# One hybrid decoder layer on one core: two blocks fewer, and the routed rows read back in three groups

## The reference, cut to what matters

```
P = x @ W_in                              # columns for three branches and three gates
A: RWKV-7 recurrence, 8 heads x 64        # S_t = S diag(w) - ..., y_t = S r_t
B: GLU -> causal conv of 31 taps -> LN -> silu
C: attention, 4 heads x 128, into 256 memory rows
h = LN(alpha*x + (sum_b sigmoid(G_b) * y_b) @ W_out)
score = sigmoid(h @ w_router); idx = top_8(score + bias) of 128 experts; gate = 2.5 * normed score
y = LN(alpha*h + shared(h) + sum_{k in idx} gate_k * w_e2[k] @ (silu(h @ w_e1[k]) * (h @ w_e3[k])))
```

## Time and profile before

| | |
|---|---|
| median of 3 runs | 1992.39 us (1991.35 to 1992.70) |
| profiled execution: its own time, its span | 1992.53 us, 1990.8 us |
| granted TensorE clock, mean | 0.951 of full |
| projections, from the span's start | to 319 us |
| recurrence | 326 to 455 us |
| merge | 455 to 753 us |
| first products of expert pair 0 / of pair 63 | 850.5 / 1901.5 us |
| final stage | 1920.8 to 1990.8 us |
| busy: TensorE, VectorE, ScalarE, GpSimd | 1783.4, 627.2, 392.3, 365.0 us |
| moved by DMA | 532 MB, mean 267 GB/s |

### The profile page before, as it was taken

One profiled execution on the slowest core, in us unless ns is written; L12 is line 12 of the kernel. 1 busy time (PEld: TensorE's weight loads), 2 busy tenths in 40 slices (PEclk: granted clock), 3 DMA queues, 4 the chain that ended last, 5 costly groups with the idle time before them and its releaser, 6 DMA issues. The chain is left out here.

```text
span 1990.8 us, 29270 instructions
## 1 busy us (share of the span) xinstructions
PE 1783.4 (90%) x10614; PEld 1047.1 (53%) x10614; DVE 627.2 (32%) x1516; ACT 392.3 (20%) x918; POOL 365.0 (18%) x529
## 2 busy tenths in 40 slices
PE   8999997998999999999988888888888888888887
PEld 6857776887778885645433333333333333333332
DVE  1387754873214312611211111111111111111127
ACT  0114544552120101311111111111111111111112
POOL 1000000888871000011110101111111111111100
PEclk8999998999999999999998989998989898989998
DMA  4443312011233324479999999999999999999965
GB/s 120 147 141 102 97 46 49 3 35 36 79 119 109 119 76 190 198 283 420 421 420 410 419 405 410 419 414 398 411 408 396 411 410 396 413 410 417 409 284 241
DMA packets 160782, 532.04 MB, mean 267 GB/s; under 512 B 22061, under 2 KB 88927, under 8 KB 110205
## 3 DMA queue, kind: packets, MB, share of 16 engines
q1 hardware_dynamic: 138921, 488.47, 62.3%
q0 software_dynamic: 20640, 41.23, 5.5%
q10 hardware_dynamic: 1148, 1.34, 0.2%
HBM read 522.52 MB, written 41.42 MB: 283 GB/s over the span
## 5 line engine op out<-in xcount | busy, mean ns | idle before, releaser
L1944 PE MATMUL bank<-arena 128*64 128x512 f32 x2048 | 513.6, 659 | 139.0 <-DMA arena<-in_w_e 137.8
L1944 PEld LDWEIGHTS bank<-arena 128*64 128x64 f32 x2048 | 159.0, 151 | 489.1 <-issue 487.7
L1962 PE MATMUL bank<-arena 128*64 128x512 f32 x1024 | 233.8, 598 | 0.0
L2187 DVE TENSOR_TENSOR arena<-bank,arena 128x256 f32<-128x256 f32 x64 | 27.2, 425 | 579.1 <-ACT arena L2032 579.1
L1812 POOL DMA_INDIRECT arena<-h_rows,index x66 | 67.1, 1016 | 772.1 <-DVE index L2061 714.2
L1431 PE MATMUL bank<-arena 128*128 128x276 f32 x768 | 184.7, 399 | 7.3 <-ACT arena L1533 3.1
L1431 PEld LDWEIGHTS bank<-arena 128*128 128x128 f32 x768 | 146.5, 191 | 41.6 <-ACT arena L1533 3.5
L2032 ACT ACTIVATE arena<-bank 128x256 f32<-128x256 f32 x64 | 24.7, 386 | 604.5 <-PE bank L1944 604.5
L1201 PE MATMUL bank<-arena 64*64 64x64 f32 (+2 forms) x2816 | 119.6, 239 | 16.4 <-DVE arena L1300 8.7
L1962 PEld LDWEIGHTS bank<-arena 128*64 128x64 f32 x1024 | 67.8, 136 | 110.9 <-issue 109.7
L1201 PEld LDWEIGHTS bank<-arena 64*64 64x64 f32 x2816 | 105.0, 135 | 22.7 <-DVE arena L1300 9.0
(11 more groups left out here) (333 smaller groups left out, 1842.3 us busy)
## 6 DMA issues: line engine op xcount, KB each, us to landing
arena<-in_w_e SPq DMA_DIRECT2D x384, 1024.0 KB, 14.2
arena<-in_w_in SPq DMA_DIRECT2D x50, 512.0 KB, 4.2
arena<-routed_rows SPq DMA_DIRECT2D x8, 2048.0 KB, 23.0
arena<-in_w_mem_kv SPq DMA_DIRECT2D x4, 1024.0 KB, 5.7
arena<-in_cache_mem_k SPq DMA_DIRECT2D x8, 512.0 KB, 4.8
arena<-in_cache_mem_v SPq DMA_DIRECT2D x8, 512.0 KB, 5.5
arena<-in_w_out SPq DMA_DIRECT2D x2, 2048.0 KB, 12.6
arena<-in_w_s SPq DMA_DIRECT2D x3, 1024.0 KB, 10.7
```

Of the source, the lines that this page charges most:

```text
L1944: mm = pe.matmul(p_gu[t * S:(t + 1) * S, :], xt[:, v, c, t * S:(t + 1) * S], w13[2 * v + t][:, :, c, :], start=(c == 0), stop=(c == KD - 1))
L1962: mm = pe.matmul(p_y[h][t * S:(t + 1) * S, :], hidT[:, j, t * S:(t + 1) * S], w2[2 * v + t][:, j, h * 512:(h + 1) * 512], start=(j == 0), ...
```

## The change

**The block.** `stage_front` becomes `front_programs`, whose five programs (unchanged but for two added signals) run at the head of the block of `stage_front_to_experts`. `recycle` and two barriers go. Explicit waits take the barrier's place:

```diff
-            pool.memset(masks[:, 3:5, :], 1.0)
+        pool.memset(masks[:, 3:5, :], 1.0).then_inc(sem("masks_ready"), 1)
...
-                    act.activation(before[:, :, 0:SEQ], rate[:, :, 0:SEQ], ACT.Exp, scale=-RATE)
+                act.activation(before[:, :, 0:SEQ], rate[:, :, 0:SEQ], ACT.Exp, scale=-RATE).then_inc(sem("decays_ready"), 1)
...
     def gpsimd(pool):
+        pool.wait_ge(sem("sample_rows"), 1)
         pool.memset(yout[:, :, SEQ:NT], 0.0)
...
+        pe.wait_ge(sem("masks_ready"), 1)
+        pe.wait_ge(sem("sample_rows_copied"), 6)
         for n in range(NCH):
             chunk(n, n % 2)
...
+        dve.wait_ge(sem("decays_ready"), 1)
         for x in range(4):
             vectors(0, 0, x)
+        dve.wait_ge(sem("masks_ready"), 1)
         chunks(dve, chunk)
...
             wkv_gpsimd(pool)
+            pool.wait_ge(m.sem("state_turned"), 1)
+            pool.wait_ge(m.sem("state_rows"), 1)
+            pool.wait_ge(m.sem("state_done"), 4 * NCH + 4)
+            for name in FRONT_ONLY:
+                pool.sem_clear(m.sem(name))
+            pool.drain()
+            pool.sem_inc(s_cleared, 1)
             pool.wait_ge(m.sem("rwkv_ready"), 1)
```

```diff
-EARLY_GROUPS = ((0, 0, 3), (0, 1, 7))
+EARLY_GROUPS = ((0, 0, 3), (0, 1, 7), (0, 2, 6))
...
+        sp.wait_ge(s_oh, 1)
+        sp.dma_start(w2s, io["w_s2"][0].rearrange("(k p) n -> p k n", p=P)).then_inc(sem("shared_down_loaded"), 16)
...
+        sp.wait_ge(s_base, 2 * NTT + 17)
+        sp.wait_ge(s_out[1], (16 * NP // 2) * count)
+        low(0)
+        sp.wait_ge(s_xt, NP * count)
+        low(1)
+        low(2)
+        sp.wait_ge(s_out[0], (16 * NP // 2) * count + 16)
+        low(3)
+        sp.wait_ge(s_gu, NP * count)
+        for i in range(NTT - 1):
+            ranks(i, O_MID, 4, 2, s_mid)
+        sp.wait_ge(s_out[1], (16 * NP // 2) * count + 16)
+        high(0)
+        high(1)
+        sp.wait_ge(s_in[1], (16 * NP // 2) * count + 16)
+        high(2)
+        sp.wait_ge(s_xt, NP * count + 1)
+        high(3)
...
+        pe.wait_ge(s_rc, NTT)
+        shared(0, 2)
+        shared(1, 2)
         count = rounds(pe)
...
-                    if v == 0:
-                        with pe.If((NP // 2) * r + i < 3):
-                            shared_late(1, i * THIRD, i + 2)
-                    else:
-                        with pe.If((NP // 2) * r + i < 4):
-                            with pe.If(i > 2):
-                                shared_late(0, 2 * THIRD, 5)
+                    with pe.If((NP // 2) * r + i < 13):
+                        if v == 0:
+                            with pe.If(i < 7):
+                                with pe.If(i > 3):
+                                    shared_late(i)
+                        with pe.If(i > 7):
+                            pe.wait_ge(s_base, 2 * i + (v + 1))
+                            for t in range(NTT):
+                                with pe.If(i < 9 + t):
+                                    with pe.If(i > 7 + t):
+                                        base(t, v)
...
+        pe.wait_ge(s_idx, NP * count + 3)
+        pe.wait_ge(s_xt, NP * count + 1)
+        pe.wait_ge(s_hc, NP * count)
+        pe.wait_ge(s_yv, NP * count + 1)
+        pe.wait_ge(s_ya, NP * count + 1)
+        for i in range(NTT - 1):
+            fold(i, O_LOW, 2, s_low)
+        for i in range(NTT - 1):
+            fold(i, O_MID, 1, s_mid)
+            fold(i, O_HIGH, 1, s_high).then_inc(s_all, 1)
```

More of the change, by code:

```diff
@@ new lines, in gpsimd @@
+    def gpsimd(pool):
+        pool.memset(restart, 1.0)
+        pool.drain()
+        pool.memset(restart[:, 0:SEQ:CH], 0.0).then_inc(sem("restart_ready"), 1)
+        pool.wait_ge(sem("key_cache_turned"), BS)
+        pool.drain()
+        for u in range(2):
+            pool.tensor_copy(qri[u][:, :, 2, :], m.fold[:, :].rearrange("p (o c) -> p o c", o=1).to_broadcast([P, KW, HD]))
+        pool.wait_ge(sem("sample_scores"), BS)
+        for h in range(2):
+            r = slice(h * HD, (h + 1) * HD)
+            pool.drain()
+            pool.tensor_copy(masks[r, 0, :], m.lower[r, r])
+            pool.drain()
+            pool.tensor_copy(masks[r, 1:3, :], m.upper[r, :, r])
+        pool.drain()
+        pool.memset(masks[:, 3:5, :], 1.0).then_inc(sem("masks_ready"), 1)
@@ L1042, in _ @@
[L1042 to L1054 removed]
+                last = dve.tensor_tensor(squares[:, j, :], kkey[:, j, :], kkey[:, j, :], ALU.mult)
@@ L1057 @@
+        n_before = TAPS - SCAN_AT
+        for k in range(n_before):
+            tap(k)
+        for q in range(N_STEP):
+            shift(q)
+            maxima(q)
+            if q < SCAN_AT:
+                tap(n_before + q)
+            normalise(q)
+            prepare(q)
+        dve.drain()
+        for j in (2, 3):
+            bonus(j)
+    return sync, gpsimd, tensor, scalar, vector
 O_SOUT = O_TOP + 2 * WEXP - KW * P
@@ L1873, in shared, with shared_late, base, fold @@
             j, third, bank = EARLY_GROUPS[g]
-            mm = shared_half(x, j, third * THIRD, bank)
+            mm = shared_half(x, j, third * THIRD, O_HT, bank)
             if x == 1:
-                mm.then_inc(s_sh, 1)
-        def shared_late(j, first, done):
-            pe.wait_ge(s_sa, done)
-            shared_half(0, j, first, 7)
-            shared_half(1, j, first, 7).then_inc(s_sh, 1)
+                mm.then_inc(s_sh, 1 + g // 2)
+        def shared_late(i):
+            pe.wait_ge(s_sa, i + 3)
+            shared_half(0, 1, i * THIRD, O_HT - 4 * THIRD, 7)
+            shared_half(1, 1, i * THIRD, O_HT - 4 * THIRD, 7).then_inc(s_sh, 1)
+        def base(t, h):
+            n, cols = RES_ROWS[t], slice(t * P, (t + 1) * P)
+            bank = m.ps[7][0:n, :]
+            for j in range(2):
+                pe.matmul(bank, sact[:, j, cols] if n == P else ssam[:, j, :], w2s[:, j, h * 512:(h + 1) * 512],
+                          start=(j == 0), stop=False)
+            for k in range(4):
+                mm = pe.matmul(bank[:, k * P:(k + 1) * P], hT[:, 4 * h + k, cols] if n == P else hsam[:, 4 * h + k, :], alpha,
+                               start=False, stop=(k == 3))
+            mm.then_inc(s_bp, 1)
+        def fold(i, place, n, s):
+            pe.wait_ge(s[i], 32)
+            for h in range(2):
+                for k in range(n):
+                    for a in range(2):
+                        part = m.at(place[i][a], n * D)
+                        mm = pe.matmul(final_bank(i, h)[a * HD:(a + 1) * HD, :], fold64,
+                                       part[:, k * D + h * 512:k * D + (h + 1) * 512],
+                                       start=(place is O_LOW and k == 0), stop=(place is O_HIGH))
+            return mm
         def find_slots(g, n, v):
@@ L2241, in _ @@
         def _(pe):
+            front_tensor(pe)
             wkv_tensor(pe)
@@ L2427, in build @@
             stage(nc, m, io)
-            if stage is stage_front:
-                m.recycle(FRONT_ONLY)
 def kernel(**inputs):
```

1484 lines of the change are left out of this document (730 added, 754 removed).

## The result

The changed kernel takes 1971.91 us (median of 4 runs, 1969.14 to 1978.12) beside 1992.34 us for the kernel before; the ratio is 0.9903, 95% interval 0.9879 to 0.9926. It is faster by 19 us (15 to 24), inside the range, but by two thirds of what was forecast. The profiled execution has a span of 1970.6 us, 20.2 less than before.

A forecast was written before the change was run, and what follows sets the result against it. The prediction took the expert loop as bound by its DMA weight stream, with gains only around it: -8.5 + 0.3 + 1.7 - 24.3 = -30.8 us from 1992.5, forecast 1962 us, range 1953 to 1975.

The forecast's parts named there:

- The boundary: Between projections and recurrence: without the two barriers and with the clears moved, the recurrence starts sooner; -8.5 us.
- Rival B: Samples' recurrence on GpSimd binds and the merge waits: boundary worth only 3 us, 1967 us; chance 10%.
- GpSimd gains 3 us: Samples' recurrence at the boundary: its reload can't start before 321, where it started at 324.46, so GpSimd gains 3 us.
- The stream's start: Ahead of the expert loop: two added matmul sets delay the first weights' request, partly regained; net +1.7 us.
- The tail: Behind the expert loop: a DMA queue, then a VectorE chain; last output at 1966.5 instead of 1990.8, -24.3 us.
- First high tile (1 MB): +2.4, 1931.7: In the tail: the first tile's high ranks land 2.4 us after the reads ahead of them, at 1931.7.
- 1902 + 4 x 0.59 = 1904.4: In the tail: end of the last weights before the change, taken from the DMA share of 0.59 from 1902 to 1906.
- the fold: In the tail: TensorE adds the first high tile in four matmuls of 0.43 us each, 1.7 us.
- Rival A: In the tail: rank reads in flight with pair 63's last weights delay them, end moves by 9 us, 1971; chance 15%.
- Rival C: In the tail: high ranks land early, low and middle ranks fitting under pair 63; up to 11 us less, about 1954; 7%.
- Rival D: In the expert loop: jumps over added code cost TensorE time beyond its room, up to 2005 us; 5% slower, 3% no difference.
- the rule on instruction fetch: TensorE's branches: taken jumps outside two pages of code would force a DMA fetch; the forecast's sum counts them as free.

The follow-up runs named there:

- e1_old_boundary: The changed kernel with the old boundary between projections and recurrence (two barriers, the clears between them): 1982.5 us, ratio 0.9952 to the kernel before.
- e3_high0_alone: The changed kernel with SP waiting until tile 0's high ranks have landed before issuing those of tiles 1 to 3 and the samples: 1972.3 us.
- e5_mids_behind: The changed kernel with the middle ranks of tiles 1 to 3 issued behind tile 0's high ranks, each before its tile's high ranks: 1963.2 us.
- e6_both: The changed kernel with e5_mids_behind's order of reads, and VectorE adding each tile before norming the previous one: 1963.7 us.
- e10_samples_second: As e6_both, with the samples' rows read right behind tile 0's high ranks and normed second: 1964.6 us.

## Why the prediction was right, and where it was not

- **Sign and place.** The gain came from the boundary and the tail, and the stretch of the loop gave next to nothing, as argued. The sum was 11 us too large (31 for 19 to 20), and the tail, one of its terms, accounts for all of that.
- **The boundary, forecast -8.5 us.** The start of the recurrence came 7.3 us sooner within the program (forecast 7.4), at full clock. Over eleven traces the gain up to the samples' turn in the merge is 8.2 us; the direct comparison of medians gives 11.0, with an interval of 4 to 21 that holds both. The clears beside the merge cost nothing that shows.
- **Rival B (GpSimd binds)** didn't come: in every run TensorE turned the samples' rows without an idle before it, 4.8 us or more after GpSimd had asked for them. The step "GpSimd gains 3 us" was too low for the profiled execution: GpSimd asked at 587.2 us instead of 596.7, 9.4 us sooner, and the slack grew instead of shrinking. From the turn of the rows to that request it took 271.8 to 277.1 us in the variants, e1_old_boundary among them with 276.4, and 281.7 before; what makes it differ is open.
- **The stream's start, forecast +1.7 us.** +4.1 up to the first pair, -2.2 inside the loop: +1.9. The first pair ran at full clock, 7.09 us for 8.75.
- **The tail, forecast -24.3 us, measured -13.0.** The step that failed is "First high tile (1 MB): +2.4, 1931.7". Less the 7.2 us by which the last pair came sooner, that is 1924.5; it landed at 1934.9, 10.4 us later. I had ended the weights where the mean share of 16 engines fell, "1902 + 4 x 0.59 = 1904.4", and had not read on: two engines worked until 1914. Whatever is read behind the weights lands by those two. The fourteen others kept to the forecast (e3_high0_alone); the lag is worth some 8 us, and the reads behind the tile another 2. A second and smaller slip is the fold: 3.7 us at half clock instead of 1.7, because TensorE had stood idle for 9.1 us. VectorE's five tiles took 29.6 us instead of 30.8, and the output 2.3 as reckoned. 10.4 + 2.1 - 1.2 = 11.3, which is the difference between -24.3 and -13.0.
- **Rival A (the reads hold up the last weights)** gave 1971, which the measured 1971.9 meets by luck and not by its mechanism: the wait ahead of the last pair was 1.09 us (1.65 before), and holding the reads back didn't shorten it.
- **Rival C (the high ranks land early)** didn't come: they landed 10.4 us late.
- **Rival D and the rule on instruction fetch.** TensorE's loop with ten more guarded pieces shows hardly an idle but the waits for weights (123.7 us of the 125.1 ahead of the pairs' products and 0.5 elsewhere; 137.8 of 139.0 before), and from the first pair to the last it took 1048.75 us instead of 1050.95. By the rule of the Trainium skill (Runtime: NRT & Kernel Launch, "Instruction fetch mechanics") the jumps over the added code could have cost a fetch each; in this loop none shows. What removing the blocks' jumps gained can't be told from what removing their barriers gained.

## What to carry to other kernels

When reads follow a long saturated stream, read the DMA share on until it is zero, not only to where it falls: here a transfer landed when the slowest of its engines was done. Order such reads by what is needed first, and keep everything else behind it. Work put ahead of a bound stream costs most of its length, however much room there is inside it.

## What the runs showed of the hardware

- Two of the 16 DMA engines end some 8 us behind the others: behind the weights in the kernel before (share 0.12 for 8 us), in the variants (0.13 for 7 and for 8 us), and behind the changed kernel's own last reads (0.13 from 1938 to 1944 us). The packet records show two packets open at a time there. Whether they are always the same two isn't shown, and what puts them behind is open. Whether the gathers and scatters are the cause wasn't tried.
- TensorE's clock after an idle. In the fourteen traces 551 pairs' products follow a wait of 0.8 us or more. They ran at full clock (7.1 us) behind 183 of 189 waits under 2 us, 20 of 56 from 2 to 3 us, 7 of 100 from 3 to 4 us, and none of 206 above; the others took 8.4 to 10.1 us. So a wait inside the stream of weights often costs more than itself, and its length alone doesn't tell: the same 3.2 us were followed by 7.09 us in e5_mids_behind and by 8.58 in the kernel before.
- The samples' read of 1 MB, in pieces of 8 KB, keeps the engines busy while they move 213 GB/s (e6_both) and 263 (e10_samples_second); stretches of the other rank reads move 404 to 409. The low ranks come in pieces of 8 KB too, so their size isn't what makes it slow.
